# Gate slabs of the second block's input projection as seven products of halves

## The reference

```python
h = _rmsnorm_2(x, g_mix[l])
proj = h @ w_in[l]
q_a, k_a, v_a, cx, cb, cc, q_m, gate_logits = jnp.split(proj, IN_SPLITS, axis=-1)
...
gates = jax.nn.sigmoid(gate_logits).reshape(b, s, N_BRANCH, d)
merged = (gates[:, :, 0] * (o_attn @ w_proj_attn[l])
          + gates[:, :, 1] * (z_conv @ w_proj_conv[l])
          + gates[:, :, 2] * (o_mem @ w_proj_mem[l]))
x = x + merged @ w_out[l]
```

## Time and profile before

| | |
|---|---|
| median of 3 runs | 2989.33 us (2986.47 to 2992.79) |
| profiled execution, own time | 2988.4 us |
| its span in the profile | 2986.5 us |
| mean granted clock of TensorE | 0.975 |
| PE busy, share of the span | 2817.0 us, 94% |
| DVE, ACT, POOL busy | 39%, 19%, 21% |
| DMA queue q1 | 631.55 MB, 56.5% of 16 engines' time |

### The profile page before, as it was taken

How to read it: one execution, slowest core, us unless ns; L and a number is a source line. 1 busy time by engine, 2 the same in 40 slices (tenths; PEclk the granted TensorE clock), 3 DMA queues, 4 the chain that set the end, 5 groups by cost and what they waited for, 6 DMA issues and landing times.

```text
span 2986.5 us, 42182 instructions
## 1 busy us (share of the span) xinstructions
PE 2817.0 (94%) x18274; PEld 2423.2 (81%) x18274; DVE 1155.4 (39%) x2204; ACT 556.1 (19%) x856; POOL 621.8 (21%) x584
## 2 busy tenths in 40 slices
PE   8999999999999999999999999999999999866766
PEld 6888988889888899899988888889988888533433
DVE  3865235452433334745214344435355312210111
ACT  2101222124211101010033116210012330100000
POOL 0001411122121075068601210038800000000000
PEclk9999999999999999999999999999999999988878
DMA  9764543344443556764544444365433328899998
GB/s 406 297 263 163 175 150 134 121 141 171 140 141 127 196 199 229 272 219 166 183 147 143 139 153 143 130 224 170 165 135 130 105 91 351 381 432 430 430 430 371
DMA packets 74155, 641.62 MB, mean 215 GB/s; under 512 B 8304, under 2 KB 9584, under 8 KB 17648
## 3 DMA queue, kind: packets, MB, share of 16 engines
q1 hardware_dynamic: 71376, 631.55, 56.5%
q10 hardware_dynamic: 2592, 7.33, 0.6%
HBM read 637.80 MB, written 1.05 MB: 214 GB/s over the span
## 4 chain that ended last, share of the span: by engine, by line
PE 86%; DMA 12%; DVE 1%; issue 0%; ACT 0%; POOL 0%; SPq 0%; DVEq 0%; POOLq 0%; ACTq 0%
PE ps L1364 27%; PE ps L1340 20%; PE ps L1386 13%; DMA work<-in_w_moe 11%; PE ps L1561 7%; PE ps L1397 3%; PE ps L1591 2%; PE ps L1374 2%; PE ps L1145 2%; PE ps L1450 1%; PE ps L1167 1%; PE ps L1568 1%; PE ps L1272 1%; PE ps L1536 0%; PE ps L1539 0%; DMA ring<-in_w 0%
## 5 line engine op out<-in xcount | busy, mean ns | idle before, releaser
L2760 POOL TENSOR_TENSOR ring<-ring 128x512 f32<-128x512 f32 (+1 forms) x294 | 374.2, 1301 | 783.0 <-DMA ring<-in_w 315.7
L1364 PE MATMUL ps<-ring 128*128 128x256 f32 x2368 | 517.4, 380 | 0.6 <-ACT ring L1784 0.6
L1364 PEld LDWEIGHTS ps<-ring 128*128 128x128 f32 x2368 | 447.3, 190 | 63.2 <-issue 2.4
L2029 DVE TENSOR_TENSOR work<-work,ps 128x128 f32<-128x128 f32 (+3 forms) x534 | 185.6, 386 | 714.6 <-PE ps L1340 349.2
L1340 PE MATMUL ps<-work,ring 128*128 128x128 f32 x3312 | 385.8, 275 | 0.3 <-POOL work L2760 0.3
L1386 PE MATMUL ps<-work,ring 128*128 128x256 f32 x1760 | 385.5, 380 | 0.0
L1340 PEld LDWEIGHTS ps<-work,ring 128*128 128x128 f32 x3312 | 377.6, 192 | 0.5 <-POOL work L2760 0.5
L1386 PEld LDWEIGHTS ps<-work,ring 128*128 128x128 f32 x1760 | 332.5, 190 | 46.2 <-issue 2.1
L1364 PE MATMUL ps<-h,ring 128*128 128x256 f32 x1408 | 310.7, 382 | 6.5 <-ACT h L1784 2.9
L1364 PEld LDWEIGHTS ps<-h,ring 128*128 128x128 f32 x1408 | 265.8, 191 | 47.0 <-issue 5.7
L2029 DVE TENSOR_TENSOR work<-work 128x128 f32<-128x128 f32 (+4 forms) x566 | 261.6, 511 | 52.1 <-ACT eb L1812 24.9
(11 more groups left out here) (315 smaller groups left out, 2655.6 us busy)
## 6 DMA issues: line engine op xcount, KB each, us to landing
ring<-in_w SPq DMA_DIRECT2D x210, 1024.0 KB, 4.9
work<-in_w_moe SPq DMA_DIRECT2D x22, 4096.0 KB, 33.5
ring<-in_w_moe SPq DMA_DIRECT2D x22, 4096.0 KB, 33.4
ring<-in_w_in SPq DMA_DIRECT2D x80, 1024.0 KB, 4.9
work<-in_w_ada SPq DMA_DIRECT2D x40, 1024.0 KB, 6.1
ring<-in_w_ada SPq DMA_DIRECT2D x32, 1024.0 KB, 5.1
ring<-in_w SPq DMA_DIRECT2D x28, 768.0 KB, 4.2
ring<-in_w_out SPq DMA_DIRECT2D x16, 1024.0 KB, 5.1
```

Of the source, the lines that this page charges most:

```text
L1364: last = nc.tensor.matmul(ps[:, b, c * L:c * L + L], w[:, k * L + c * P:k * L + c * P + P], hs[cols][:, k, :], start=(k == 0), stop=(k == ...
L2029: return nc.vector.tensor_tensor(o, i0, i1, op)
L2760: return nc.gpsimd.tensor_tensor(o, i0, i1, ALU.subtract)
```

## The change

The twelve gate slabs of the second block's input become halved slabs. What that involves:

- `HALVED_IN2` lists them, `run_of` makes them one run, and `with_halves` is now applied to the whole plan, so that "halves" and "combine" stages appear in the second block too; the ring has four places from three slabs ahead of the run to its end.
- PE issues seven products of four 128-column matmuls a slab.
- ACT's evacuation with the sigmoid (one instruction from PSUM) becomes: a copy of one product in the course of the slab, and the sigmoid from the sums in on-chip memory, behind DVE's five additions.
- The token sums, the third combination and the partial sums lie in space of the merged branches and of work tiles that is free meanwhile (`in2_halves`, `in2_mixed4`, `in2_sums`). SP therefore waits for the last gate before it fetches one of the experts' slabs there.
- Waits on a slab of the input go through `given`, which knows whether ACT or DVE delivered it; the target views are gathered in `in2_target`.

```diff
+HALVED_IN2 = [('gt', 0), ('gt', 1), ... ('gt', 11)]
...
+    if stage[0] == "in2" and stage[1:] in HALVED_IN2:
+        return ("in2",)
...
-        if run[0] != "down":
+        if run[0] == "in2":
+            before[at].append(("halves", 0, run))
+        elif run[0] != "down":
...
-    return with_halves(with_inverses(plan)) + second_order()
+    return with_halves(with_inverses(plan) + second_order())
...
+        in2_sums = shaped(work[:, 1536:1536 + 10 * P], 2, 5, P)
+        in2_mixed4 = [shaped(work[:, 4608 + i * 4 * P:4608 + i * 4 * P + 4 * P], 4, P) for i in range(2)]
+        in2_halves = [shaped(work[:, 5632 + i * 4 * P:5632 + i * 4 * P + 4 * P], 4, P) for i in range(4)]
...
+                        if i == 2:
+                            sp.wait_ge(*given("gt", 11))
...
-                            h_ready(KD - 1)
-                            h_seen = max(h_seen, 8 * at.h_norms[n])
-                            s1, s2, s3, s4 = z_halves if kind == "z" else halves
-                            (a11, a12), (a21, a22) = quarters_of_tokens(hs[stage[2]])
+                            if kind != "in2":
+                                h_ready(KD - 1)
+                                h_seen = max(h_seen, 8 * at.h_norms[n])
+                            s1, s2, s3, s4 = {"z": z_halves, "in2": in2_halves}.get(kind, halves)
+                            (a11, a12), (a21, a22) = quarters_of_tokens(hs[0 if kind == "in2" else stage[2]])
...
-                        nc.scalar.activation(part_sums[:, which, 1, :], ps[:, at.group[n] % 4, 2 * P:3 * P], ACT.Copy
+                        five = (in2_sums if kind == "in2" else part_sums)[:, which]
+                        nc.scalar.activation(five[:, 1, :], ps[:, at.group[n] % 4, 2 * P:3 * P], ACT.Copy
                                              ).then_inc(one_out, 1)
...
+                        elif kind == "in2" and stage[1] == "gt":
+                            act.wait_ge(ev_d, at.sums_at[n])
+                            nc.scalar.activation(in2_target(stage), five[:, 1:5, :].rearrange("p (c t) n -> p c (t n)", c=2),
+                                                 ACT.Sigmoid).then_inc(ev_a, 1)
...
-                        dve.wait_ge(h_done, 8 * at.h_norms[n])
+                        if run[0] == "in2":
+                            dve.wait_ge(x2_done, KD)
+                        else:
+                            dve.wait_ge(h_done, 8 * at.h_norms[n])
```

More of the change, by code:

```diff
@@ L53 @@
 HALVED_DOWN = [(1, 0, 0), (1, 0, 1)]
+HALVED_IN2 = [('gt', 0), ('gt', 1), ('gt', 2), ('gt', 3), ('gt', 4), ('gt', 5), ('gt', 6), ('gt', 7), ('gt', 8), ('gt', 9), ('gt', 10), ('gt', 11)]
 LENT = 4
@@ L455, in __init__ @@
                     self.count_hid(stage)
+                elif kind == "in2":
+                    if stage[1] != "gt":
+                        self.in2_at[stage[1:]] = ("d", self.d)
+                    else:
+                        self.a += 1
+                        self.in2_at[stage[1:]] = ("a", self.a)
+                        set_read[self.set_of[n]] = self.a
+                    set_freed[self.set_of[n]] = self.d
                 elif copied_z(stage):
@@ L492, in __init__ @@
                 self.freed[self.group[n]] = ("a", self.a)
-                self.in2_at[stage[1:]] = self.a
+                self.in2_at[stage[1:]] = ("a", self.a)
             elif kind == "hsum":
@@ L882, in weights_of, with given @@
             return parts_of(w, DOWN_K[stage[5]] // 2) if stage[0] == "down" else quarters_of(w)
+        def given(*slab):
+            engine, count = at.in2_at[slab]
+            return (ev_a if engine == "a" else ev_d), count
         def made(*z):
@@ L896, in mixed_of @@
             n = DOWN_K[stage[5]] // 2 if stage[0] == "down" else 4
+            if stage[0] == "in2":
+                return m[:, :, 0, :], m[:, :, 1, :], in2_mixed4[nth % 2]
             return m[:, 0:n, 0, :], m[:, 0:n, 1, :], mixed4[run_of(stage) in ((0, 1, 0), (1, 1, 0))][nth % 2][:, 0:n, :]
@@ L932, in z_target, with in2_target @@
             return dst[:, c:c + 2, :], func
+        def in2_target(stage):
+            what, j = stage[1:]
+            if what == "va":
+                return va[:, :, j * L:j * L + L]
+            view = {"qk": qk, "qm": qm, "cx": cx[:, 0], "cb": cx[:, 1], "cc": cx[:, 2], "gt": gt}[what]
+            return view[:, 2 * j:2 * j + 2, :]
         units = [("a", s, t) for s in range(4) for t in range(2)] + [("m", s, t) for s in range(4) for t in range(2)]
@@ L1647, in first @@
                         if u == 0:
-                            pe.wait_ge(ev_a, at.in2_at["va", 2])
+                            pe.wait_ge(*given("va", 2))
                         pe.wait_ge(un_pt, u + 1)
@@ L1888, in first @@
                         b = done()
[L1889 to L1898, removed]
+                        nc.scalar.activation(in2_target(stage), ps[:, b, :].rearrange("p (c n) -> p c n", c=2),
+                                             ACT.Sigmoid if stage[1] == "gt" else ACT.Copy).then_inc(ev_a, 1)
                     elif kind == "nsquare":
@@ L1901, in first @@
                         if i < 6:
-                            act.wait_ge(ev_a, at.in2_at["qk", i])
+                            act.wait_ge(*given("qk", i))
                         elif i >= 8:
-                            act.wait_ge(ev_a, at.in2_at["qm", i - 8])
+                            act.wait_ge(*given("qm", i - 8))
                         if i >= 2:
@@ L2159, in first @@
                         s, run = stage[1:]
-                        s1, s2, s3, s4 = z_halves if run[0] == "z" else halves
+                        s1, s2, s3, s4 = {"z": z_halves, "in2": in2_halves}.get(run[0], halves)
                         (a11, a12), (a21, a22) = quarters_of_tokens(hs[s])
-                        before = [r for r, i in at.halves_at.items() if i < at.halves_at[run] and (r[0] == "z") == (run[0] == "z")]
+                        before = [] if run[0] == "in2" else [r for r, i in at.halves_at.items() if i < at.halves_at[run] and (r[0] == "z") == (run[0] == "z")]
                         if before:
@@ L2175, in first @@
                         which, bx, by = at.set_of[n], at.group[n] % 4, (at.group[n] + 1) % 4
-                        five = part_sums[:, which]
+                        five = (in2_sums if kind == "in2" else part_sums)[:, which]
                         c1, c2 = (five[:, 1:5, :].rearrange("p (c t) n -> p c t n", t=2)[:, :, t, :] for t in range(2))
                         to1, to2 = c1, c2
+                        if kind == "in2" and stage[1] != "gt":
+                            to1, to2 = (in2_target(stage)[:, :, t * P:t * P + P] for t in range(2))
                         if kind == "z" and copied_z(stage):
@@ L2507, in first @@
                         two = slice(2 * j, 2 * j + 2)
-                        dve.wait_ge(ev_a, at.in2_at["cb", j])
+                        dve.wait_ge(*given("cb", j))
                         u, w = cx[:, 0], cx[:, 2]
@@ L2548, in first @@
                         if j == 0 and what == "pa":
-                            dve.wait_ge(ev_a, at.in2_at["gt", 11])
+                            dve.wait_ge(*given("gt", 11))
                         if what == "pa":
```

## The result

The changed kernel takes 2996.88 us (median of 7 runs, 2994.93 to 2998.12) against 2988.04 us for the kernel before (7 runs): ratio 1.0027, 95% interval 1.0018 to 1.0037. It is slower, by 0.27%.

What follows compares the result with a forecast made beforehand. TensorE, busy 94% of the span, was taken to bound the kernel through the gate stretch. Stalls of 11.2 + 0.6 + 2.1 = 13.9 us less 7.9 saved gave +6.0 to +6.1: 2995.4 us, range 2991 to 3000.5.

Steps and rivals of the forecast that it cites:

- positions 23 to 29: Gate slabs 3 to 9 with the attention work behind each: turns at 2.71 us instead of 1.11, 11.2 us of stalls.
- the chain of sums, sigmoid and copy: Behind a halved gate slab: ACT starts at 1.77 us, mix copy runs 2.30 to 2.57, turns start at 2.71 us.
- The saving: On PE, each of twelve gate slabs takes 6.25 us instead of 6.91: 0.66 us x 12 = 7.9 us saved.
- Position 22: Gate slab 2 and the work behind it, with a long-form mix: turns at 2.61 instead of 1.99 us, 0.6 us stall.
- Position 21: Gate slab 1 and the work behind it: 0.6 us plus 1.5 for sums delayed by the convolution, 2.1 us stall.
- the mean row of 1.45 us: Trace figure for a two-input SBUF operation of DVE beside POOL, 1.45 us instead of 0.69; used for the last convolution step.
- The evacuation of the gate slab is thus on the path: Kernel before, positions 23 to 29: the evacuation holds the turns through ACT's queue, ahead of the mix copy; turns 1.11 us.
- The table load: ACT's 1.28 us load, taken as hidden in the slab; rival, chance 0.04: it stands behind the sums, +12.4 us on top.
- The late DVE: Rival, chance 0.08: position 20's convolution and softmax steps double under POOL, the convolution ends 4 us later: +10, 2999.4 us.
- The turns were held: Against the rival, chance 0.07, that the mix copy reaches PE as early as before: only the saving left, -7.9 us, 2981.5.
- the row count given for the opposite: Support for the rival that turns are not held: seven of nine such positions show no wait put down to ACT.
- the 0.2% line: What a measurement can tell from no change, 6 us, line at 2995.3; chances slower 0.50, within 0.43, faster 0.07.

Runs made afterwards that it cites:

- e_wait_in_mix: Changed kernel, with TensorE's wait for the earlier mix's copy moved, for short-form units, from before the turns to before its own mix: 2983.8 us, ratio 0.9981.
- e_two_sigmoids: Changed kernel with each gate sigmoid done twice, the second after the first has ended: 3004.72 us, ratio 1.0043.

## Why the prediction was right

**The sign and the mechanism: shown.** The forecast was +6.1 us, 2995.4; measured were +8.8 us and 2996.88 in the first comparison. That the time came within 1.5 us is in part luck: the median before, 2989.33 from three runs, was 2988.04 with seven, and the lower start hid half of the 2.7 us that the difference was short. Turns at 2.71 us were forecast for positions 23 to 29, 2.71 to 2.72 came; the chain of sums, sigmoid and copy has each member where it was put (sigmoid at 1.78 us, copy at 2.31 to 2.57, forecast 1.77 and 2.30 to 2.57). Turning round two instructions of ACT took the loss away, doubling one of them added to it one to one, and moving the wait on PE took it away at positions 22 to 29 as the new order on ACT did.

**The saving: shown.** 6.25 us a slab, 12 x 0.655 = 7.9 us. Three slabs alone gave 2.02.

**Position 22: 0.76 us instead of 0.6.** With a long unit's copy (half the partitions) ACT started after the sigmoid's end (2388.30 + 0.63, copy at 2388.95) and not 0.1 us before it.

**Position 21: 2.46 us instead of 2.1.** The sum had taken 1.5 us for the convolution's delay between 0.6 and 1.9. The multiply took 1.75 us, near the 1.94 of being locked out for a whole POOL operation and far from its undisturbed 0.69; the sums started 1.7 us late, and 0.76 + 1.70 is the 2.46. The Trainium skill (SBUF — State Buffer, "Who interferes with whom") has the two-input VectorE instruction wait for the whole of a GpSimd instruction that reads SBUF; 1.75 or 1.76 us here, in six kernels, agrees better with that than the mean row of 1.45 us did. POOL's three operations beside it took 4.17 us instead of 3.72, so both sides were held up.

**The clock: a term that was missing.** The sum ended with the stalls, 13.9 us forecast and 14.5 found. That a gap of 2.1 to 2.3 us on PE can be followed by some 3 us at half the clock (windows of 8 us over such slabs show 0.79 to 0.83), which cost 1.6 us each time (part of it in the turns ahead of the slab), was not in it. Of the three profiles of the changed kernel none, two and one slab fell. With it the stretch is 6.6, 9.8 and 8.2 us longer in the three profiles, and the medians lie 8.8, 8.4 and 6.9 us over the kernel before. How much of these the clock makes stays open, as said above.

**"The evacuation of the gate slab is thus on the path": wrong as a statement on the kernel before.** It lost 0.04 us to it. That the turns waited for the copy was right: without the wait they come 0.88 us after the mix, and 0.44 at position 29 (e_wait_in_mix). But the copy's own way, 1.07 us from mix to turns, was the limit; the evacuation just fitted in ahead of it. The queue had no slack left, and that is what the forecast needed: the price of the new work, counted from 1.11 us, came out right for this reason and not for the one given.

**The rivals.** The table load stayed in the slab (2392.83 to 2394.11, the sigmoid starts at 2397.69). It takes 1.28 us, and behind such a load the exponential starts 0.02 us later (load at 2389.24, exponential at 2390.54); no longer figure for a switch was met. The late DVE costs 1.7 us once and not 4. The turns were held; the row count given for the opposite was off by one (of positions 21 to 29 eight, not seven, show no wait put down to ACT before the change), and nothing in the sum hung on it. A time beyond the 0.2% line had been given 0.50 and came.

## What to carry to other kernels

When a faster form of a matmul needs more steps to evacuate its result, ask on each engine what stands in the queue behind the new wait, not who needs the result: here nobody was in a hurry for the gates, and a 0.27 us copy behind them cost 14.5 us. Such a loss is mended by order alone; the same change with the copy first is 0.26% faster instead of 0.27% slower. A gap of 2.1 to 2.3 us on TensorE can cost another 1.6 us behind it, in some executions, through the clock.

## What the runs showed of the hardware that was not expected

The clock fell behind single gaps of 2.1 to 2.8 us, and not each time. Behind gaps of 1.67 us, six in a row in four profiles, no slab was slow. In e_two_sigmoids, with gaps of 2.33 us at positions 23 to 28 and 2.76 us at 29, three of seven slabs were. What decides which is open; the profiles show only that the same kernel goes one way or the other.
